# Norms of a two-block model: root ahead of the split, first outputs side by side, squares in the preceding stage

## The reference

```python
def _rmsnorm(h, g):
    h32 = h.astype(jnp.float32)
    y = h32 * lax.rsqrt(jnp.mean(h32 * h32, axis=-1, keepdims=True) + NORM_EPS)
    return (y * g.astype(jnp.float32)).astype(h.dtype)

def _modnorm(h, g, shift, scale):
    return _rmsnorm(h, g) * (1.0 + scale) + shift

def _ffn_half(h, g, shift, scale, gate, w_in, w_out):
    a, b = jnp.split(_modnorm(h, g, shift, scale) @ w_in, 2, axis=-1)
    return h + 0.5 * gate * ((jax.nn.silu(a) * b) @ w_out)
```

## Time and profile before

| what | value |
|---|---|
| median of 3 runs | 3714.63 us (3710.47 to 3714.92) |
| profiled execution | 3717.88 us, of which the span is 3716.1 us |
| TensorE matmuls busy | 3304.6 us, 89% of the span |
| VectorE, ScalarE, GpSimd busy | 40%, 31%, 5% |
| granted TensorE clock, mean | 0.942 of full |
| HBM traffic | 623.98 MB by DMA, 421 GB/s in the Moe stages, 167 GB/s over the span |

### The profile page before, as it was taken

How to read it: one execution, slowest core, us unless ns; L and a number is a source line. 1 busy time by engine, 2 the same in 40 slices (tenths; PEclk the granted TensorE clock), 3 DMA queues, 4 the chain that set the end, 5 groups by cost and what they waited for, 6 DMA issues and landing times. The chain is left out here.

```text
span 3716.1 us, 54738 instructions
## 1 busy us (share of the span) xinstructions
PE 3304.6 (89%) x24132; PEld 2544.8 (68%) x24132; DVE 1478.5 (40%) x2702; ACT 1139.4 (31%) x1787; POOL 180.1 (5%) x338
## 2 busy tenths in 40 slices
PE   4778887899899779997999988999989998898898
PEld 3767766555499664544777765777767876777898
DVE  3545555322344542224333234333243334325554
ACT  2434443221244331113222223222232223124443
POOL 1022220000000000000000000000000000000000
PEclk7888998899899989998999989999989998999899
DMA  5233332699666119993444413444322222212352
GB/s 213 91 121 107 124 121 109 251 421 421 265 238 238 54 53 420 421 421 127 159 153 152 161 61 114 149 176 159 119 80 85 102 85 108 68 46 102 137 185 100
DMA packets 106574, 623.98 MB, mean 168 GB/s; under 512 B 11744, under 2 KB 14176, under 8 KB 47968
## 3 DMA queue, kind: packets, MB, share of 16 engines
q1 hardware_dynamic: 69760, 485.62, 34.2%
q0 software_dynamic: 36576, 134.85, 10.1%
HBM read 619.37 MB, written 1.05 MB: 167 GB/s over the span
## 5 line engine op out<-in xcount | busy, mean ns | idle before, releaser
L334 PE MATMUL ps<-t,t 128*128 128x512 f32 (+1 forms) x3520 | 1252.0, 356 | 162.3 <-DVE t L449 73.5
L335 PE MATMUL ps<-t,t 128*128 128x512 f32 (+1 forms) x3520 | 1225.8, 348 | 0.0
L336 PE MATMUL ps<-t,t 128*128 128x512 f32 (+1 forms) x3520 | 1225.0, 348 | 0.0
L310 DVE TENSOR_TENSOR t<-t,t 128x1024 fp32r<-128x1024 f32 x452 | 550.7, 1224 | 823.9 <-ACT t L300 821.9
L334 PEld LDWEIGHTS ps<-t,t 128*128 128x128 f32 x3520 | 679.2, 193 | 287.8 <-issue 107.9
L335 PEld LDWEIGHTS ps<-t,t 128*128 128x128 f32 x3520 | 681.5, 194 | 83.9 <-issue 2.9
L336 PEld LDWEIGHTS ps<-t,t 128*128 128x128 f32 x3520 | 680.0, 193 | 85.6
L300 ACT ACTIVATE t<-t 128x1024 fp32r<-128x1024 f32 x452 | 473.7, 1054 | 630.6 <-PE ps L336 611.1
L1047 PE MATMUL ps<-t,t 128*64 128x512 f32 x1248 | 302.6, 595 | 9.7 <-DMA t<-in_experts_dram 9.7
L1047 PEld LDWEIGHTS ps<-t,t 128*64 128x64 f32 x1248 | 120.2, 137 | 183.3 <-issue 147.7
L547 POOL DMA_DIRECT2D t<-in_wmod_dram x240 | 126.8, 534 | 1569.2 <-PE ps L498 1567.1
(11 more groups left out here) (291 smaller groups left out, 3042.8 us busy)
## 6 DMA issues: line engine op xcount, KB each, us to landing
t<-in_experts_dram SPq DMA_DIRECT2D x234, 1024.0 KB, 13.5
t<-in_wall_dram SPq DMA_DIRECT2D x221, 1024.0 KB, 4.9
t<-in_wmod_dram POOLq DMA_DIRECT2D x240, 512.0 KB, 5.8
t<-in_wall_dram SPq DMA_DIRECT2D x10, 512.0 KB, 3.6
t<-in_lora_dram POOLq DMA_DIRECT2D x8, 512.0 KB, 3.9
t<-in_rcst_dram POOLq DMA_DIRECT2D x1, 1536.0 KB, 6.5
t<-in_x_dram SPq DMA_DIRECT2D x1, 1024.0 KB, 12.4
t<-in_ctx_dram POOLq DMA_DIRECT2D x1, 1024.0 KB, 5.9
```

What stands on the lines that cost most here:

```text
L310: e.tensor_tensor(lo, self.raw(n), hi, ALU.subtract).then_inc(*net.wlo.up((self.name, n)))
L334: e.matmul(out, lh, rh, start=start, stop=False, **kw)
L335: e.matmul(out, lh, rl, start=False, stop=False, **kw)
L336: return e.matmul(out, ll, rh, start=False, stop=stop, **kw)
```

## The change

The norm's parts get an order of their own, in stages that have both a norm and weights (`act_with` and `dve_with` in AttnIn, Ffn and RetIn). ScalarE parts one chunk, makes the root, parts more and then shifts. VectorE makes the mean, parts one chunk, makes the reciprocal, and parts one further chunk behind every second scaling.

TensorE's first outputs (three in AttnIn, four in Ffn and RetIn) run side by side in as many banks, as the norm's chunks come. AttnIn, the final norm and Ffn (0,0) become early norms; for Ffn (0,0) the context's half is squared in the last four pairs of Moe 1 (the context is loaded there, on GpSimd's queue, once the routing has used that room), the other half behind the final norm's scalings. Fourier's columns wait only for their own chunk. RetIn makes the 512-wide outputs first and its decay constants later. AttnIn calls the background job ahead of each output instead of behind it.

```diff
+def side_by_side(e, w, net, ws, norm, uses, T):
+    wts, bs, done = [], [], [0] * len(uses)
+    for k in range(8):
+        for x, use in enumerate(uses):
+            if k < x:
+                continue
+            if len(wts) == x:
+                wts.append(ws.pe(w))
+                bs.append(net.banks.take(w, use))
+            norm.ready(w, k)
+            for c in range(done[x], k + 1):
+                m = mm3(e, net.ps[:, bs[x], 0:T], both(wts[x], c), net.U(c, 0, T), c == 0, c == 7)
+            done[x] = k + 1
+            if k == 7:
+                m.then_inc(*net.sums.up(use))
+                ws.used(x)
...
     def pe(self, e, w):
-        for c in range(7 if self.early else 0, 8):
+        for c in {False: range(8), True: (7,), "all": ()}[self.early]:
             self.pe_square(e, w, c)
 
-    def dve_root(self, e, w):
+    def dve_root(self, e, w, ws=None):
         net = self.net
         b, r = net.banks.of((self.name, "square")), net.rstd[:, 0:self.T]
         w.wait_ge(*net.sums.of((self.name, "square", 7)))
         e.tensor_scalar(r, net.ps[:, b, 0:self.T], 1.0 / 1024, 1e-6, ALU.mult, ALU.add).then_inc(*net.vecs.up((self.name, "mean")))
         net.banks.emptied((self.name, "square"), net.vecs, (self.name, "mean"))
+        if ws:
+            ws.dve_to(e, w, 1)
         w.wait_ge(*net.acts.of((self.name, "root")))
         e.reciprocal(r, r).then_inc(*net.vecs.up((self.name, "rstd")))
...
+    def act_with(self, e, w, ws, side):
+        if not self.early:
+            for c in range(8):
+                self.act_square(e, w, c)
+        ws.act_to(e, w, 1)
+        self.act_sqrt(e, w)
+        ws.act_to(e, w, min(side, 2 * len(self.halves)))
+        for n in range(self.n):
+            self.act_apply(e, w, n)
+            ws.act_to(e, w, min(side, 2 * len(self.halves) + (n + 1) // 2))
+        ws.begun()
+
+    def dve_with(self, e, w, ws, side):
+        self.dve_root(e, w, ws)
+        self.dve_gain(e, w)
+        for n in range(self.n):
+            if n > 1:
+                self.dve_low(e, w, n - 2)
+            self.dve_scaled(e, w, n)
+            if n % 2:
+                ws.dve_to(e, w, min(side, 1 + (n + 1) // 2))
+        self.dve_low(e, w, self.n - 2)
+        self.dve_low(e, w, self.n - 1)
+        ws.begun_low()
...
@@ Moe.pe, in the loop over pairs, g == 5 in the last four @@
             if g < 5:
                 self.pe_gather(e, w, g, k + 1, 3)
+            elif self.ctx:
+                for c in (k, k + 1):
+                    self.ctx().pe_square(e, w, c)
             self.pe_down(e, w, p)
         self.pe_scatter(e, w, self.PAIRS - 1)
+        for o in range(7):
+            self.following().pe_square(e, w, o)
@@ Moe.act @@
+            if g == 5 and self.ctx:
+                w.wait_ge(net.s_ctx, 16)
+                for c in (k, k + 1):
+                    self.ctx().act_square(e, w, c)
...
+        for o in range(8):
+            w.wait_ge(*self.of(net.vecs, "added", o))
+            self.following().act_square(e, w, o)
@@ Moe.pool @@
+        if self.ctx:
+            w.wait_ge(*self.of(net.sums, "tokens", 3))
+            e.dma_start(net.XW[:, :, 256:512], net.args["ctx"]).then_inc(net.s_ctx, 16)
@@ PlainNorm.act and, likewise with pe_square, PlainNorm.pe @@
+        if self.following:
+            for c in range(8):
+                w.wait_ge(*net.vecs.of((self.norm.name, "normed", c)))
+                self.following().act_square(e, w, c)
@@ Ffn.pe @@
+        side_by_side(e, w, net, ws, self.norm, [self.key + (0, y, z) for y in range(2) for z in range(2)], T)
         for ph in range(2):
             for y in range(11):
                 for z in range(2):
+                    if ph == 0 and y < 2:
+                        continue
@@ Ffn.dve @@
-        ws.dve(e, w)
-        self.norm.dve(e, w)
+        self.norm.dve_with(e, w, ws, 4)
@@ Fourier.pe @@
-                    w.wait_ge(*self.norm.all_kept())
+                    w.wait_ge(*net.acts.of((self.norm.name, "kept", 2 * g + 1)))
@@ RetIn @@
+    ORDER = list(range(8, 16)) + list(range(8))
+        side_by_side(e, w, net, ws, self.norm, [("rqk", n) for n in self.ORDER[:4]], 512)
@@ stages @@
-    add(Moe, 0)
+    add(Moe, 0, at(4))
-    add(Moe, 1)
+    add(Moe, 1, at(8), lambda: net.stages[9].squares[1])
-    add(PlainNorm, "final", ctx=True)
-    add(Ffn, 0, 0, 512, False, at(10))
+    add(PlainNorm, "final", lambda: net.stages[9].squares[0])
+    add(Ffn, 0, 0, 512, "all", at(10))
```

More of the change, by code:

```diff
@@ L368, in pe_square @@
         if c == 0:
-            self.b = net.banks.take(w, (self.name, "square"))
+            self.b = net.banks.take(w, (self.name, "square"), self.at)
             net.banks.kept.add(self.b)
@@ L458, in all_kept, with __init__, key, sq @@
         return self.net.acts.of((self.name, "kept", self.n - 1))
+class Squares:
+    def __init__(self, norm, c0, first):
+        self.norm, self.c0, self.first = norm, c0, first
+    def key(self, c):
+        return (self.norm.name, "half square", self.c0, c)
+    def sq(self, c):
+        return self.norm.net.sq[c % 2][:, self.c0:self.c0 + 256]
+    def act_square(self, e, w, c):
+        net = self.norm.net
+        if c > 1:
+            w.wait_ge(*net.sums.of(self.key(c - 2)))
+        e.activation(self.sq(c), self.norm.xc(c)[:, self.c0:self.c0 + 256], ACT.Square).then_inc(*net.acts.up(self.key(c)))
+    def pe_square(self, e, w, c):
+        norm, net = self.norm, self.norm.net
+        if c == 0 and self.first:
+            norm.b = net.banks.take(w, (norm.name, "square"), norm.at)
+            net.banks.kept.add(norm.b)
+        w.wait_ge(*net.acts.of(self.key(c)))
+        e.matmul(net.ps[:, norm.b, self.c0:self.c0 + 256], net.c("ones"), self.sq(c), start=(c == 0), stop=(c == 7)).then_inc(
+            *net.sums.up(self.key(c)))
+        if c == 7 and not self.first:
+            net.sums.note((norm.name, "square", 7))
+            net.banks.kept.discard(norm.b)
 class Mods:
@@ L2014, in pe @@
         self.norm.pe(e, w)
+        side_by_side(e, w, net, ws, self.norm, [("qk", 0, o) for o in range(3)], 256)
         for g in range(3):
             for o in range(16):
+                net.bg_pe.go(e, w, 0.26)
+                if g == 0 and o < 3:
+                    continue
                 use = ("qk", g, o)
@@ L2020, in pe @@
                 for k in range(8):
-                    self.norm.ready(w, k)
                     m = mm3(e, net.ps[:, b, 0:256], both(wt, k), net.U(k, 0, 256), k == 0, k == 7)
@@ L2313, in __init__ @@
         self.ws = net.stream(self.key, specs, bufs)
-        self.norm = Norm(net, ("norm",) + self.key, T, lambda c: net.XW[:, c, 0:T], halves, early=early)
+        self.norm = Norm(net, ("norm",) + self.key, T, lambda c: net.XW[:, c, 0:T], halves, early=early, at=3 if early == "all" else None)
+        self.squares = [Squares(self.norm, 256 * y, y == 1) for y in range(2)]
     def pe(self, e, w):
@@ L2632, in act @@
         net, ws = self.net, self.ws
[L2633 to L2639 removed]
+        self.norm.act_with(e, w, ws, 4)
+        for x, n in enumerate(self.ORDER):
+            if x:
                 ws.act(e, w)
```

202 lines of the change are left out of this document (100 added, 102 removed).

## The result

| | before | changed |
|---|---|---|
| median, 4 runs each | 3714.78 us (3710.47 to 3719.97) | 3670.78 us (3669.15 to 3672.60) |
| ratio, 95% interval | | 0.9881 (0.9862 to 0.9899) |
| profiled execution, span | 3717.88, 3716.1 us | 3672.60, 3670.8 us |
| mean granted clock | 0.942 | 0.945 |

The change brought 44.0 us; the forecast was 38.8 us, 3676 us, in a range of 3660 to 3696.

What follows compares the result with a forecast made beforehand. TensorE, busy nearly nine tenths of the span, was taken as the bound, with time to win only where it idles or runs at half clock. Stage gains summed to 38.8 us: 3714.6 to 3675.8 (3676), range 3660 to 3696.

Steps and rivals of the forecast that it cites:

- Side by side: Ffn, RetIn, AttnIn: first outputs together as chunks come; four 512-wide ones end 27.2 us behind the first matmul.
- The forecast's own bound for no half clock: Side-by-side outputs: four wide ones take 25.2 us without half clock; as a rival 3660 us, chance 0.07.
- The rivals with a late clock: First outputs: clock returns later, four take 30.2 us (3695, chance 0.17), or half clock throughout (3756; slower 0.03).
- Root first: Norm heads of Ffn, AttnIn, RetIn: reciprocal 3.8 us earlier, first matmul 2.7 us (five buffers: 4.9 and 3.8).
- Behind the four: Wait for the fifth output: TensorE idles 0.7 us, RetIn 1.15; in Ffn (0,1) fifth output 3.6 us behind.
- AttnIn: AttnIn: squares ride the eight adds, first matmul 2.7 us earlier, three outputs side by side; gain 4.5 us.
- Moe 1 to Ffn (0,0): Context's squares cost Moe 1 2.4 us in pairs 18 and 19; fifth output of Ffn (0,0) gains 8.7, that paid.
- Bare table loads: Five table loads losing their cover: rival has each cost twice its length, 1.28 us more; 3682 us, chance 0.04.
- Fourier: Columns start as chunks come: rows 1.0 us earlier, but half clock after a pause costs 2 to 3.5; taken -1.0.
- The wait of L346 for L517: Sign: TensorE's idle time before products that ends with a low part of a norm falls from 73.5 to about 45 us.
- That of squares: Sign: TensorE's idle time before squares that ends with a square made on ScalarE falls from 42.8 to under 10 us.

Runs made afterwards that it cites:

- f: Changed kernel with one line undone, so that Fourier's columns wait for the whole norm again; ran once, 3675.4 us.
- h: Changed kernel with TensorE's background steps behind the four side-by-side outputs put ahead of the fifth and sixth output, one each; ran once, 3670.3 us.
- i: Changed kernel with three repairs: Fourier's columns wait for the whole norm, context's squares behind down, background steps apart; 3668.5 us, 0.9866 of before.
- w: Changed kernel with idle matmuls ahead of each group of side-by-side outputs (18 in wide stages, 12 AttnIn, 13 Ffn (1,1)); 3661.7 us, 0.9868 of before.
- j: Kernel i plus idle matmuls ahead of the side-by-side outputs and three more behind the first and second chunk in 512-wide stages; 3653.5 us, 0.9838 of before.
- the eight profiles: Profiles of kernels with the changed norm order and side-by-side outputs, without idle matmuls, changed kernel twice among them; four 512-wide outputs took 25.8 to 27.3 us.
- b: Changed kernel with its first outputs one after another again, root-first order kept; 3706.9 us, 0.9976 of before.
- c: Changed kernel with both the root-first order and the side-by-side outputs undone; 3708.6 us, 0.9972 of before.
- g: Changed kernel with the context's squares of Moe 1 pairs 16 to 19 on TensorE behind down instead of ahead; ran once, 3675.4 us.

## Why the prediction was right, step by step

**Side by side.** The forecast had 27.2 us from first matmul to the end of four, of it half clock until 9 us. Measured: 26.0 to 26.5 to the start of the last matmul, half clock until 6.4 to 7.8. This is the term that was too large, by about 1 us in each wide stage. What was off was when the clock returns, and not what it costs: where the half clock did last until 8.3 to 9.1 us (f, h, i), the four took 27.0 to 27.3. The forecast's own bound for no half clock was 25.2; w measured 25.2 in Ffn (1,0), j 25.6 to 25.8. The rivals with a late clock needed 16 us or more of it; no wide stage of the eight profiles had it beyond 9.1.

**Root first.** Forecast: first matmul 2.7 us (five buffers 3.8) earlier. Measured behind the last square: 12.60 to 9.33 in Ffn (0,1), 3.3; 13.72 to 9.47 in Ffn (1,0), 4.2; 10.93 to 6.95 in Ffn (1,1), 4.0. The reciprocal starts 2.4 us behind the last square instead of 6.5, so 4.1 earlier and not 3.8. The 0.5 us too few and up to 1.2 us of the clock explain Ffn (0,1) and Ffn (1,0) (5.95 and 8.67 for 4.5 and 7.8) and RetIn (9.72 for 8.3); in Ffn (1,1) the fifth output follows at 13.3 us, not 14.6.

**Behind the four.** Forecast 3.6 us in Ffn (0,1), measured 3.76 from the start of the last matmul. In RetIn the split keeps the fifth output waiting for 0.81 us, 1.15 forecast:

```profile
3112.45 0.50 PE L346 MATMUL ps<-t,t 128*128 128x512 f32 x1 [0.81 <-DVE t L323]
```

**AttnIn.** 4.5 as forecast. From the first add of Moe 0, the first matmul comes at 15.1 us (17.4 before) and the fifth output 16.4 us behind it (18.6 before), so half of the gain lies in each. Undone from the changed kernel, the early squares cost 0.4 us, the side-by-side outputs 2.6 (b), those and root first together 2.7 (c, both from the last square); with the last two undone the stretch is still 1.9 us under before. How much of the 4.5 is the squares' isn't settled. That the sum fits to 0.1 us is luck: with the squares at full clock (h, i) the gain was 6.3.

**Moe 1 to Ffn (0,0).** 2.7 us lost in Moe 1, 2.4 forecast, by the mechanism named: pairs 16 and 17 hide the squares, 18 and 19 lose 1.4 us each, and g gives 1.5 back by place alone. The stretch gained 10.2 for 8.7, again by the head and the four outputs.

**Bare table loads.** The rival in which each costs twice its length fell:

```profile
1696.14 1.28 ACT L434 ACT_TABLE_LOAD   x1 [1.65 <-DVE t L418]
1697.43 0.42 ACT L434 ACTIVATE t<-t 128x256 f32<-128x256 f32 x1
```

The root starts 1.29 us behind the load's start. The Trainium skill (ScalarE: Activation LUTs, What ACT_TABLE_LOAD costs) charges 2.66 us; this row says 1.28, and the measurement decides. The 1.65 us of idle time ahead of this load could hide something, but the loads ahead of the root in AttnIn, Ffn (1,0), RetIn and Ffn (1,1) start 0.02 us behind a split, and the root follows 1.29 to 1.30 us behind their start.

**Fourier.** Forecast +1.0 for the earlier rows and -2 to -3.5 for the clock, taken -1.0. The rows came 0.95 us earlier behind the last square (22.51 to 21.56), but f has the same 21.55 with the old wait: that microsecond is the norm's order, not this line's. The line itself is a pure loss of 2.6 us, by the clock.

**Named signs that failed.** The wait of L346 for L517 was to fall to about 45 us and is 54.2: I left out that a head still takes 8.7 to 9.2 us in four stages. That of squares was to fall below 10 and is 22.7, since I had overlooked that 14.8 of it is a wait at the program's start that no norm in these stages has.

## What to carry to other kernels

When a producer delivers an operand in chunks and one consumer output needs all of them, run several outputs side by side: it was worth over half of the gain here, and moving the head of the producer forward paid nearly twice as much with it as without (13.2 against 7.2 us by stage). Ask of a low clock where it lies before pricing it: in a stretch where TensorE waits for chunks it costs little (up to 2 us for up to 9 us of half clock), and ahead of dense work (Fourier's rows) an "earlier start" that ends in a pause costs more than it wins. A step that is moved under cover needs its cover named for every iteration: two of four pairs had none.

## What the runs showed that I had not expected

- RwkvCore alone varied by 10.9 us between two profiled executions of one program, while the stretches of the table agreed within 0.3 us. A difference of a few microseconds is read from stages; and one of about 1 us in a stage only with the granted clock beside it, since the four outputs scatter from 25.8 to 27.3 us with where the half clock ends.
- Idle matmuls in a wait hold the granted clock at 1.00 (0.61 in the same wait without them), and in three of four wide stages of w it was lost again behind the first chunk, though the wait had been filled.
- Squares made early on ScalarE bring little where TensorE sums them at half clock: 7.2 us for eight, 0.4 us won at the end. At full clock eight took 5.25 us, and the end came 1.9 us earlier still.
